# Six pairs of feed-forward gate tiles computed by seven products, with three groups instead of two

## The reference

```
n2 = _rms(h, norm_ffn_w[l])
up = _causal_dwconv(n2 @ w_up[l], ffn_dw_w[l], ffn_dw_b[l])   # 3 taps over tokens
gate, val = jnp.split(up, 2, axis=-1)                         # 2816 columns each
h = h + (jax.nn.silu(gate) * val) @ w_down[l]
```

## Time and profile before

| what | value |
|---|---|
| three timed runs | 1825.46, 1825.42, 1823.94 us |
| median | 1825.42 us |
| profiled execution | 1825.35 us, of which the span of its instructions 1823.5 us |
| granted TensorE clock, mean | 0.998 |
| TensorE busy | 1806.2 us |
| VectorE busy | 1343.2 us |
| ScalarE busy | 923.2 us |
| GpSimd busy | 128.6 us |

### The profile page before, as it was taken

How to read it: one execution, slowest core, us unless ns; L and a number is a source line. 1 busy time by engine, 2 the same in 40 slices (tenths; PEclk the granted TensorE clock), 3 DMA queues, 4 the chain that set the end, 5 groups by cost and what they waited for, 6 DMA issues and landing times.

```text
span 1823.5 us, 32958 instructions
## 1 busy us (share of the span) xinstructions
PE 1806.2 (99%) x13774; PEld 1724.5 (95%) x13774; DVE 1343.2 (74%) x2370; ACT 923.2 (51%) x1792; POOL 128.6 (7%) x110
## 2 busy tenths in 40 slices
PE   9999999999999999999999999999999999999998
PEld 8999999978899998999899999999899999999987
DVE  5888897678757773566688887978458888787844
ACT  6222333568734442343456666666446566666632
POOL 0000000000000000000011121211000111111000
PEclk9999999999999999999999999999999999999999
DMA  5222222201132223222357777775332677677431
GB/s 196 93 88 75 93 93 70 93 24 38 57 99 93 87 71 120 93 84 75 98 118 155 165 154 161 157 151 124 119 105 76 124 157 159 152 156 157 113 125 69
DMA packets 229474, 202.46 MB, mean 111 GB/s; under 512 B 5846, under 2 KB 225807, under 8 KB 229326
## 3 DMA queue, kind: packets, MB, share of 16 engines
q1 hardware_dynamic: 177566, 174.67, 31.0%
q0 software_dynamic: 51744, 25.70, 11.4%
q10 hardware_dynamic: 16, 0.00, 0.0%
HBM read 198.25 MB, written 2.10 MB: 110 GB/s over the span
## 4 chain that ended last, share of the span: by engine, by line
PE 90%; ACT 4%; DVE 4%; issue 1%; DMA 0%; DVEq 0%; SPq 0%; ACTq 0%
PE ps L195 63%; PE ps L199 25%; PE ps L204 2%; ACT p L207 1%; DVE wlo L210 1%; DVE ast L1071 1%; ACT whi L207 1%; DVE mxl L210 0%; DMA xt<-in_x_dram 0%; ACT nhi L207 0%; ACT L207 0%; ACT pa L207 0%; ACT at L207 0%; ACT ps L207 0%; DVE na L210 0%
## 5 line engine op out<-in xcount | busy, mean ns | idle before, releaser
L210 DVE TENSOR_TENSOR wlo<-raw,whi 128x1024 fp32r<-128x1024 f32 (+1 forms) x357 | 424.0, 1191 | 257.2 <-ACT whi L207 255.8
L207 ACT ACTIVATE whi<-raw 128x1024 fp32r<-128x1024 f32 (+1 forms) x357 | 367.2, 1030 | 262.4 <-PE ps L195 221.4
L195 PE MATMUL ps<-nhi,whi 128*128 128x256 f32 (+3 forms) x1840 | 405.9, 288 | 2.6 <-DVE clo L210 0.8
L195 PE MATMUL ps<-nhi,wlo 128*128 128x256 f32 (+3 forms) x1840 | 402.4, 287 | 0.0
L195 PE MATMUL ps<-nlo,whi 128*128 128x256 f32 (+3 forms) x1712 | 364.9, 286 | 0.0
L195 PEld LDWEIGHTS ps<-nhi,whi 128*128 128x128 f32 x1840 | 296.2, 189 | 6.7 <-DVE clo L210 1.0
L195 PEld LDWEIGHTS ps<-nhi,wlo 128*128 128x128 f32 x1840 | 295.7, 189 | 2.1
L195 PEld LDWEIGHTS ps<-nlo,whi 128*128 128x128 f32 x1712 | 270.8, 189 | 1.9
L199 PE MATMUL ps<-thi,whi 128*128 128x256 f32 x784 | 224.8, 287 | 1.4 <-DVE wlo L210 0.8
L199 PE MATMUL ps<-thi,wlo 128*128 128x256 f32 x784 | 221.6, 283 | 0.0
L199 PE MATMUL ps<-tlo,whi 128*128 128x256 f32 x784 | 221.4, 282 | 0.0
(11 more groups left out here) (325 smaller groups left out, 3182.9 us busy)
## 6 DMA issues: line engine op xcount, KB each, us to landing
raw<-in_w_in_dram SPq DMA_DIRECT2D x90, 1024.0 KB, 5.7
raw<-in_w_up_dram SPq DMA_DIRECT2D x22, 1024.0 KB, 5.0
raw<-in_w_out_dram SPq DMA_DIRECT2D x20, 1024.0 KB, 5.0
s1t<-in_w_in_dram SPq DMA_DIRECT2D x49, 256.0 KB, 3.2
s1t<-in_w_in_dram POOLq DMA_DIRECT2D x49, 256.0 KB, 7.2
raw<-in_w_in_dram POOLq DMA_DIRECT2D x49, 256.0 KB, 4.7
raw<-in_w_down_dram SPq DMA_DIRECT2D x8, 768.0 KB, 4.4
raw<-in_w_down_dram SPq DMA_DIRECT2D x8, 640.0 KB, 4.0
```

The source lines that it names most:

```text
L195: return pe.put(after, lambda e: e.matmul(o, w, m, start=start, stop=stop_), mark)
L207: return ac.put(after, lambda e: e.activation(o, i, func, **kw))
L210: return dv.put(after, lambda e: e.tensor_tensor(o, a, b, op))
```

## The change

Six of the gate columns, j = 5 to 10, are computed by `seven`, which becomes a general function (width 258, with one column in both token halves: `SPAN`). For that the tokens have to be sums of normalised tokens: `scale_tokens_again` writes the normalised tokens over `nhi` and `nlo` in the first down product, by 8 products `nf<-h,cv,rbc` on VectorE, four sums `sf` of 128x1032, eight splits, and later four splits of the sums (`shi`, `slo`). From the second group on PSUM is then only copied (by ScalarE) instead of multiplied by `rbc`. The groups become columns 0 to 3, 4 to 7 and 8 to 10, with three down products of 8 slots each (`DOWN`); `loose` is emptied at the end of each up group and, but for the last, of each down product. Tiles use the four pairs of banks in turn before; now it is three pairs in the first group and in the down products and two in the other up groups (`ring[1]`), and the sevens use banks 6, 7 and 4.

```diff
-        GROUPS = [(0, 6), (6, 11)]
+        SEVEN = [(0, KT, 0, 128, 0), (0, 4, 0, 128, 1), (0, 4, 0, 256, 2), (4, 8, 0, 256, 3)]
+        SEVEN_AT = [0, 4, 1, 2]
+        GROUPS = [(0, 4), (4, 8), (8, 11)]
+        DOWN = [(0, 0), (1, 0), (0, 1), (1, 1), (2, 0), (2, 1), (3, 0), (3, 1)]
+        GATES_BY_SEVEN = range(5, 11)
+        first_ffn = len(plan)
         for a, b in GROUPS:
             for j in range(a, b):
-                unit(cols(w_up[0], 256 * j), BY_K if j == 0 else BY_COL)
+                unit(cols(w_up[0], 256 * j), BY_K if j == 0 else SEVEN if j in GATES_BY_SEVEN else BY_COL)
                 unit(cols(w_up[0], FF + 256 * j), BY_COL)
             n = b - a
-            for j in range(4):
-                for i in range(2):
-                    unit(cols(w_down[0], 256 * j, 2 * a + n * i, n),
-                         [(0, 3, 0, 256), (3, n, 0, 256)])
-        first_layer = len(plan)
-        first_slot_of_layers = sum(len(ss_) for _, ss_ in plan)
-        place = [(s - first_slot_of_layers) % 3 for s in range(first_slot_of_layers)]
+            for j, i in DOWN:
+                unit(cols(w_down[0], 256 * j, 2 * a + n * i, n), [(0, n, 0, 256)])
+        turns = [[n != 1 or ss_ is not SEVEN for n in range(len(ss_))] for _, ss_ in plan]
+        turns = [t for ts_ in turns for t in ts_]
+        place = [(sum(turns[:s]) - sum(turns)) % 3 if t else 4 for s, t in enumerate(turns)]
         swaps = [(1, 2)]
...
+        def seven(dst, banks, after, hook, direct, summed_, used, width=256):
+
+
+            s0 = taken[0]
+            taken[0] += 4
+
+            def slot(i):
+                fill(s0 + i + 1)
+                return ready[s0 + i]
+
+            ah, al, ta = slot(0)
+            left, right = slice(0, 128), slice(128, 256)
+            A, B, C = [P[:, 512 * b:512 * b + width] for b in banks]
+            d11, d12 = dst[0][:, 0:width], dst[0][:, width:2 * width]
+            d21, d22 = dst[1][:, 0:width], dst[1][:, width:2 * width]
+
+            def product(o, wh, wl, t_w_, x, start, stop_, after_):
+                xh, xl, tx = x
+                for k in range(4):
+                    for i, (w, m) in enumerate(((wh, xh), (wh, xl), (wl, xh))):
+                        t = mm_on([t_w_ if k + i == 0 else None, after_ if k + i == 0 else None, tx[k] if i == 0 else None], o,
+                                  w[:, k, :], m[:, k, :], start and k + i == 0, stop_ and k == 3 and i == 2, mark=k == 3 and i == 2)
+                return t
+
+            t = product(A, ah[:, 0:4, :], al[:, 0:4, :], ta, direct(0, 0), True, True, claim(banks[0]))
+            s1 = act([t, after[0]], d11, A, ACT.Copy)
+            hook(0)
+            t = product(B, ah[:, 4:8, :], al[:, 4:8, :], ta, direct(1, 0), True, True, claim(banks[1]))
+            done(t, s0)
+            c11 = tt([t, s1], d11, B, d11, ALU.add)
+            release(c11, banks[1])
+            hook(1)
+            bh, bl, tb = slot(2)
+            t = used[0] = product(A, bh[:, :, left], bl[:, :, left], tb, summed_(0), False, True, s1)
+            u2 = act([t], d12, A, ACT.Copy)
+            hook(2)
+            ch, cl, tc = slot(1)
+            t = used[1] = product(C, ch, cl, tc, summed_(1), True, True, claim(banks[2]))
+            done(t, s0 + 1)
+            k5 = act([t, after[1]], d22, C, ACT.Copy)
+            hook(3)
+            t = used[2] = product(A, bh[:, :, right], bl[:, :, right], tb, summed_(2), False, True, u2)
+            done(t, s0 + 2)
+            u3 = act([t], d21, A, ACT.Copy)
+            c22 = stt([k5, u3], d22, d22, -1.0, d21, ALU.mult, ALU.subtract)
+            hook(4)
+            dh, dl, td = slot(3)
+            t = product(C, dh[:, :, left], dl[:, :, left], td, direct(1, 1), False, True, k5)
+            c12 = tt([t, u2], d12, C, d12, ALU.add)
+            release(c12, banks[2])
+            hook(5)
+            t = used[3] = product(A, dh[:, :, right], dl[:, :, right], td, summed_(3), False, True, u3)
+            done(t, s0 + 3)
+            c21 = act([t, c22], d21, A, ACT.Copy, scale=-1.0)
+            release(c21, banks[0])
+            hook(6)
+            return [[c11, c12], [c21, c22]]
...
+            scaled = [False]
+
+            def next_y():
                 n = nth[0] % 5
                 nth[0] += 1
-                zr, y = ZR[n], Y[n]
-                a = tt([t, st["r"], zr_used[n]], zr, z, rbc[:, 0:TQ], ALU.mult)
+                return n
+
+            def up_out(z, t, banks, j, atok, jl):
+                n = next_y()
+                if scaled[0]:
+                    a = act([t, zr_used[n]], ZR[n][:, 0:TQ], z, ACT.Copy)
+                else:
+                    a = tt([t, st["r"], zr_used[n]], ZR[n][:, 0:TQ], z, rbc[:, 0:TQ], ALU.mult)
                 release(a, *banks)
-                b = act([a, t_vec, y_used[n]], y, zr[:, 0:T2], ACT.Identity, bias=cf[:, 132 + j:133 + j], scale=cf[:, j:j + 1])
+                up_taps(n, a, j, atok, jl, Y[n], lambda i: ZR[n][:, i:i + T2])
+                loose_run(2 if scaled[0] else 1)
+
+            def up_seven(j, atok, jl):
+
+                ns = [next_y(), next_y()]
+
+                def hook(m):
+                    tick(1)
+                    if m in (2, 5):
+                        step()
+
+                t = seven([ZR[n] for n in ns], [6, 7, 4], [zr_used[n] for n in ns], hook,
+                          lambda r, c: (NHI[:, 4 * r:4 * r + 4, SPAN[c]], NLO[:, 4 * r:4 * r + 4, SPAN[c]], ntok[4 * r:4 * r + 4]),
+                          lambda i: (SHI[i], SLO[i], [stok[i]] * 4), [None] * 4, width=258)
+                for c, n in enumerate(ns):
+                    z = ZR[n].rearrange("p (h t) -> p h t", h=2)
+                    up_taps(n, t[c], j + c, atok, jl + c, Y[n].rearrange("p (h t) -> p h t", h=2), lambda i, z=z: z[:, :, i:i + 256], False)
+
+            def up_taps(n, ready_, j, atok, jl, y, z, steps=True):
+                b = act([ready_, t_vec, y_used[n]], y, z(0), ACT.Identity, bias=cf[:, 132 + j:133 + j], scale=cf[:, j:j + 1])
...
+            stok = [None] * 4
+
+            def scale_tokens_again(read):
+
+
+                x = [[NF[:, 4 * r:4 * r + 4, SPAN[c]] for c in range(2)] for r in range(2)]
+                tk = {}
+                for f in range(KT):
+                    tk["f", f] = stt([read, st["r"]], NF[:, f, 0:TQ], H[:, f, Q0:T1], cv[:, f, WFFN:WFFN + 1], rbc[:, 0:TQ], ALU.mult, ALU.mult)
+
+                def sum_(i, a, b, op, after):
+                    tk["s", i] = tt([read, after], SF[i], a, b, op)
+
+                def high(f):
+                    tk["h", f] = act([tk["f", f]], NHI[:, f, 0:TQ], NF[:, f, 0:TQ], ACT.Copy)
+
+                def low(f):
+                    d = tt([tk["h", f], [tk["s", i] for i in range(4)]], NLO[:, f, 0:TQ], NF[:, f, 0:TQ], NHI[:, f, 0:TQ].bitcast(F), ALU.subtract)
+                    ntok[f] = [tk["h", f], d]
+
+                def sum_high(i):
+                    tk["sh", i] = act([tk["s", j] for j in range(4)], SHI[i], SF[i], ACT.Copy, scale=-1.0 if i == 0 else 1.0)
+
+                def sum_low(i):
+                    if i == 0:
+                        d = stt([tk["sh", i]], SLO[i], SF[i], -1.0, SHI[i].bitcast(F), ALU.mult, ALU.subtract)
+                    else:
+                        d = tt([tk["sh", i]], SLO[i], SF[i], SHI[i].bitcast(F), ALU.subtract)
+                    stok[i] = [tk["sh", i], d]
+
+                first = [lambda: sum_(1, x[0][0], x[0][1], ALU.subtract, [tk["f", f] for f in range(4)]),
+                         lambda: sum_(2, x[1][1], x[0][1], ALU.subtract, [tk["f", f] for f in range(8)]),
+                         lambda: sum_(0, SF[1], x[1][1], ALU.add, tk["s", 1]),
+                         lambda: sum_(3, SF[0], x[1][0], ALU.subtract, tk["s", 0])]
+                first += [lambda: high(0), lambda: high(1)]
+                for f in range(KT):
+                    first += [lambda f=f: low(f)] + ([lambda f=f: high(f + 2)] if f + 2 < KT else [])
+                rest = [lambda: sum_high(1), lambda: sum_high(2)]
+                for i, j in ((1, 0), (2, 3), (0, None), (3, None)):
+                    rest += [lambda i=i: sum_low(i)] + ([lambda j=j: sum_high(j)] if j is not None else [])
+                return first, rest
+
             for g, (ja, jb) in enumerate(GROUPS):
-                atok = [None] * 12
+                atok = [None] * 8
+                ring[1] = 2 if g else 3
                 for j in range(ja, jb):
                     if j == 0:
                         zs = two_tiles(([pair_dst(TQ), pair_dst(TQ)], HALVES), NHI, NLO, ntok)
                         ffn_stats()
+                    elif j in GATES_BY_SEVEN:
+                        up_seven(2 * j, atok, 2 * (j - ja))
                     else:
-                        zs = []
                         for c in range(2):
                             z = tile(TQ, NHI, NLO, ntok)
                             up_out(*z, 2 * j + c, atok, 2 * (j - ja) + c)
```

(34 more changed lines are left out.)

104 lines of the change are left out of this document (21 added, 83 removed).

## The result

The changed kernel takes 1865.22 us (median of six runs, 1861.60 to 1869.33) against 1824.67 us before (six runs): 1.0225 times as long, 95% interval 1.0210 to 1.0239. The profiled execution took 1864.46 us with a span of 1862.5, so 39.1 us more than the profiled one of before.

The account below looks back on a forecast made before the run. TensorE's gapless matmuls were taken to bound the kernel, each wait costing its full length: -8.6 + 9.25 + 10.5 + 3.8 + 13.3 + 3.4 = +31.7 on 1825.35 us gave 1857 us, own range 1850 to 1864; 1838 to 1868 held 0.84.

Parts of the forecast that it names:

- the four places: Predicted TensorE waits: the fourth slot of the first down product, the sevens' third product, start of j = 4, layer 0.
- Part 1: Gate columns by sevens: 72 matmuls fewer at 0.119 us each, -8.6 us.
- Part 2: First down product: fourth slot's `wlo` queued behind rotary steps, `nf` products and sums, +10.5 us; bounds 0.8 and 13.
- the walk: Step-by-step count of VectorE's queue in the first down product: fourth `wlo` ready at 26.7 us, wanted at 16.6.
- Part 3: Sevens' third product: `wlo` behind `c11` in five of six, 1.85 us each, +9.25 us; bounds nothing and 11.1.
- The 784 rows of its lower bound: Sevens' lower bound of nothing: 784 first products in the layers lost 0.8 us in all to `wlo`.
- the weights' extra sums: Weight sums on POOL and by accumulating DMA, ordered two units ahead, taken as costing nothing.
- Part 4: Start of j = 4: banks 0 and 1 wait for `h` steps behind the third slot's split, +3.8 us; range 1.4 to 4.
- part 5: Start of layer 0: first matmuls wait for `h` 6 and 7 to free banks, +13.3 us; bounds 0 and 17.
- Part 6: Clock falling behind the two waits of about 10 and 13 us, 1.7 us each, +3.4 us; bounds 0 and 5.4 each.
- the one with the clock or late weights: Rival: clock stays low a slot or more after each wait, or weights land late; 1864 us and above, chance 0.08.
- the rival that all hides: Rival: boundary waits hide; 1826 us with the sevens' waits (chance 0.04), 1817 us without (0.08).

Follow-up runs that it names:

- all_mended: Changed kernel with sevens' splits before the first product, rotary steps and token normalising spread, h before third split, four bank pairs, four last-down steps per slot: 1830.35 us.
- perfected: `all_mended` plus sevens' third split before the last value tile's steps, second weight sum ordered with the first, token sums split in the first down product: 1821.76 us.
- banks_first: Changed kernel with the two h steps ahead of the third slot's split at the end of the first and second down product: 1860.00 us.
- last_banks: Changed kernel whose last down product takes four pairs of banks in turn from pair 0, so its last pair is banks 6 and 7: 1860.55 us.
- split_first: Changed kernel with the split for the feed-forward sevens' third product queued ahead of the first product and ScalarE's copy of it: 1862.61 us.
- split_ahead: Changed kernel with the split for the feed-forward sevens' third product queued ahead of `c11`: 1864.61 us.

## Why the prediction was right, and where not

The forecast was 1857 us, +31.7, and it came to +39.1 by the profiled runs, 1865.22 us by the median: inside the range 1838 to 1868, just above the forecast's own 1850 to 1864. Direction, the four places and what holds TensorE at each were right; the clock was mis-sized and one wait was missed. Parts 1 to 5 together were forecast at 28.25 us and came to 27.5, with misses of up to 1.1 us that partly cancel. Each part against its measure:

| part | predicted | measured |
|---|---|---|
| 1, matmuls removed | -8.6 | -8.2 |
| 2, first down product | +10.5 | +9.7 (0.23 + 9.44) |
| 3, third product of the sevens | +9.25 | +10.1 (1.88, 3.30, three of 1.65) |
| 4, start of j = 4 | +3.8 | +3.7 |
| 5, start of layer 0 | +13.3 | +12.2 (10.40 + 1.75) |
| 6, clock | +3.4 | +8.9, or +7.2 less the 1.7 of before |
| not forecast: `zr` at 548.56 | 0 | +1.8 |

- Part 1 was worked out with the step of the tiles, 0.119 us; a seven's matmuls all have 258 columns and take 10.08 / 84 = 0.120.
- Part 2 stood on nearest rows; `nf` took 0.67 a step and the sums 1.17, against the 0.67 and 1.2 taken from the earlier trace rows. Its lower bound does not come out: the rotary steps take 6.0 us in the walk and the `nf` products 5.4, and without them 26.7 falls to 15.3, ahead of the 16.2 wanted, so the bound was nothing lost. The edit that moves them proves the order, and shows the fall of the wait to 2.07 us.
- Part 3 had the place and nearly the price, 1.65 for 1.85 (with the matmul's end, 0.16, which the forecast counts in, 1.81), but its mechanism was half of it. `c11` is on the way, as said; that it could be taken out and the wait would go was wrong, since ScalarE's `whi` behind its own copy takes nearly as long. The 784 rows of its lower bound are not first products but, by their name `thi`, matmuls of the four products with sums of tokens, the third among them, so the bound stands. The sentence that costs the weights' extra sums at nothing failed, too: at j = 6 the DMA of the weights' sum was late and cost 1.65 us more than at the other sevens in after, and 2.1 us more in `all_mended`. That it was late because it was ordered behind a raw load is argued: `perfected`, which orders it earlier, has no wait there, but carries two other edits. It is the cover that the prediction named, gone in one seven of six.
- Part 4 and part 5 held in mechanism and size. Without the split part 4 came to 0.82 us in `banks_first`, below its bound of 1.4; the sum of part 5, as written, is 13.4 and not 13.3. The lower bound of part 5, banks free and nothing lost, would not have held: `last_banks` shows 7.0 us left when the banks are free and the steps stand as in after.
- Part 6 is the term that was mis-sized. It counted two waits, of ten us and more; four were followed by low clock, those of 3.71 and 3.30 us as well, and each cost 1.7 to 2.6 us. The row it was read from the earlier trace rows, 1.7 us, is the smallest of these. The Trainium skill ("TensorE: Matmul & The Clock Gate", Part 1: The HAM clock gate) has it that throttled is the default and activity releases it; the trace of after agrees behind these four waits and shows no fall behind five others of 1.65 to 1.88 us. The term should have been weighed for every wait of some us, not for the two long ones.
- The wait for `zr` comes from the three pairs of banks in the first group in place of four: the first tiles of j = 0 hold theirs until the inverse norms are there. `all_mended`, with four pairs among its edits, has no wait there; no run changes the pairs alone. The section on the change names the three pairs, and the walk began behind them.

Of the rivals, the one with the clock or late weights (1864 us and above, 0.08) describes what was added to the forecast, and its time is nearer than that of the forecast. What the prediction says for the rival that all hides, VectorE busy for under half of the down windows, holds for the first (24.42 of 55 us) and not for the second (34.69 of 54).

## What to carry to other kernels

On an engine that works in order, a change that adds work is priced by what stands behind that work, not by the engine's busy share: all of the 37 us of waits came although VectorE is idle for a quarter of the span, and nearly the same instructions in another order, with another turn of the banks, took all but 1.7 us of them away. When a wait is found, follow every queue that feeds it to the same depth before pulling one link out, and look at the next link. Where TensorE has run without a gap, add to each new gap of some us a stretch of low clock as a possible cost, and compare traced executions only after taking out what each lost to the clock elsewhere.

## What the runs showed of the hardware

The clock was not expected to fall behind short waits. In every trace with a wait of 9 us or more it stood at 0.50 behind it. Behind shorter ones it fell in some executions and not in others: behind 3.71 us in after but not in `split_first`, behind 3.30 us in after but not behind 3.05 in `split_ahead` or 3.00 in `all_mended`, behind 1.82 us in `banks_first` (0.50 at 551 us) but not in after (1.00). Low clock that costs 1.6 to 3.3 us also stood at 9 us or at 372 to 374 us, far from the change, in the traces of all kernels but after.

That goes with the spread. The six runs of after span 7.7 us, and their mean granted clock is 0.992 in the fastest and 0.987 and 0.989 in the two slowest; the four of `last_banks` span 7.3 us, with 0.996 in the fastest and 0.991 in the two slowest. The six runs of before span 1.5 us, two later series of it 3.7 and 5.0 us. That the clock makes all of the spread is not shown, since one execution of each kernel was traced.
